# Three 2x2 block products with seven products each, in six of the eight ffn stages of a two-model transformer kernel

## The chip, the cores and the metric

The kernel runs on one core of a Trainium2 chip. The metric is the device time of one execution in microseconds (us); lower is better. A core has a matrix engine (PE, TensorE), two engines for elementwise work (DVE, VectorE, and ACT, ScalarE), GpSimd (POOL), a queue engine (SP, SyncE) that here only issues DMAs, and 16 DMA engines that all queues share.

## The reference, cut to what matters

The reference runs two small transformer models one after another on 256 tokens of width 1024, in float32: four blocks with eight feed-forward layers (ffn), and between these an HGRN2 mixer, forgetting attention (fox), a short convolution and sparse attention with compressed keys (kv, nsa). The change touches the ffn layers:

```python
def rmsnorm(x, g):
    y = x32 * lax.rsqrt(jnp.mean(x32 * x32, axis=-1, keepdims=True) + EPS)
    return (y * g.astype(jnp.float32)).astype(x.dtype)

def swiglu(h, w_in, w_out):
    gate, up = jnp.split(h @ w_in, 2, axis=-1)
    return (jax.nn.silu(gate) * up) @ w_out
...
x = x + 0.5 * swiglu(rmsnorm(x, norm_g[layer, 0]), ffn_w_in[layer, 0], ffn_w_out[layer, 0])
```

`w_in` is 1024 x 5632 (2816 gate columns, then 2816 up columns), `w_out` is 2816 x 1024.

## The kernel before, in words

The tokens are two tiles of 128 (t = 0, 1), the width is eight tiles of 128 (k). An ffn stage f (0 to 7) walks over 11 chunks c of 256 hidden columns. Each float32 factor is split in two parts, hi (rounded by ACT, `w_hi_`) and lo (the rest, subtracted by DVE, `w_lo_`), and a product is three matmuls: hi*hi, hi*lo, lo*hi.

One chunk is this:

- SP loads 2 MB of `w_in` (256 gate and 256 up columns) into `raw_in`, in halves of four k, as soon as the chunk in front has been split, and 1 MB of `w_out` into `raw_out`.
- ACT and DVE split each half (lines 435 and 445), 128x2048 elements at a time.
- PE does the first product for t = 0 and t = 1, 24 matmuls of 512 columns each, into `bank[t]` (lines 421 to 423).
- ACT takes silu of the gate half (line 792) and DVE multiplies it with the up half into `h_` (line 839; in the code `read(t)`). PE waits for the h of chunk c-1 before it writes the bank again.
- PE turns h by four transposes (`turn`, line 699), ACT and DVE split the turned h (lines 785 and 831), and `w_out` is split too (lines 798 and 844, `weights_out`).
- PE does the second product (`second`, 24 matmuls, lines 718 to 720), which adds into four accumulator banks. The second product of chunk c-1 comes behind the first product of chunk c.

Every engine runs its own list in the order in which the code is written, and waits on semaphores that others raise (`w_hi`, `w_lo`, `h`, `prod`, `ht_lo`, `wo_lo`). There is no scheduler. A load waits only for its buffer. At a stage's end the last chunk's `w_out` is split in halves (lines 814 and 859), and x is updated (line 868).

Of the kernel before, what the change touches and what calls it, by code (L numbers as in the profile page):

```python
# [8 lines left out]
ACT = mybir.ActivationFunctionType  # L9
# [5 lines left out]
P = 128  # L15
# [22 lines left out]
ARENA = 14336  # L38
# [34 lines left out]
M_FOX, M_NSA = 3 * NCH, 7 * NCH + 1  # L73

# [46 lines left out]
ns_csub ns_cexp ns_cp ns_cturned ns_cpt ns_cpv ns_co ns_turned13  # L121
own_act own_dve own_pool
# [21 lines left out]
class Memory:  # L144
    def __init__(self, nc, stack, t):
# [11 lines left out]
        self.wh = sb("w_hi_", [P, 2, KT, CW], F32R)  # L157
        self.wl = sb("w_lo_", [P, 2, KT, CW], F32R)
# [18 lines left out]
        self.lbs = sb("lower_bound_", [P, 2, KT])  # L177
        self.arena = sb("arena", [P, ARENA])
# [10 lines left out]
        for src, w in self.source:  # L189
            so_far = [so_far[p] + len(src(p)) for p in range(2)]  # L190
            self.land.append([16 * n for n in so_far])
# [16 lines left out]
    def piece(self, tile, n, half, k=None):  # L208

        w = self.source[n][1]  # L210
        if k is None:
            return tile[:, n % 2, 4 * half:4 * half + 4, 0:w]
        return tile[:, n % 2, 4 * half + k, 0:w]
# [131 lines left out]
def sp_program(g, sp):  # L345
    def chunk(n):
        if n == N_ALL:
            return
        src, w = g.source[n]
        for half in range(2):  # L350
            sp.wait_ge(g.w_lo, 8 * (n - 1) + 4 * half + 4)
# [6 lines left out]

    chunk(0)
    weights, f = ffn_weights(g.t), 0  # L360
    for s, kind in enumerate(STAGES):
        if kind == "ffn":
            w_out = weights[f][1].rearrange("(c k p) n -> c p k n", p=P, k=FC // P)
            for c in range(NCH):
                if f == 7 and c == 1:
                    sp.wait_ge(g.ns_turned, 2 * NSA_HEADS)
                if c:
                    out(m_of(f, c - 1), g.raw_out[:], w_out[c - 1])
                chunk(N0[s] + c + 1)
            out(m_of(f, NCH - 1), g.raw_out[:], w_out[NCH - 1])  # L370
# [6 lines left out]
        for c in range(CHUNKS[kind]):  # L377
            chunk(N0[s] + c + 1)
# [16 lines left out]
def pe_product(g, pe, n, t, out, u, w=CW, feature_major=False, slot=None, both=False):  # L395
# [3 lines left out]
    def operands(k):  # L399
        pe.wait_ge(g.w_lo, 8 * n + 4 * (k // 4) + 4)  # L400
        pe.wait_ge(g.xt_lo, 16 * u + pieces_for(u, t, k, feature_major, both))

    wh, wl, par = g.wh, g.wl, n % 2
    tok = slice(t * P, (t + 1) * P)
    mm = pe.e.matmul
    for f in range(2 if feature_major else 1):
        c = slice((2 * t + f) * P, (2 * t + f + 1) * P)
        for k in range(KT):
# [5 lines left out]
            if feature_major:  # L414
                o = out[:, f * T:(f + 1) * T]
                mm(o, wh[:, par, k, c], xt_hi[:, k, :], start=first, stop=False)  # L416
                mm(o, wh[:, par, k, c], xt_lo[:, k, :], start=False, stop=False)  # L417
                last = mm(o, wl[:, par, k, c], xt_hi[:, k, :], start=False, stop=end)  # L418
            else:
                o = out[:, 0:w]  # L420
                mm(o, xt_hi[:, k, tok], wh[:, par, k, 0:w], start=first, stop=False)  # L421
                mm(o, xt_hi[:, k, tok], wl[:, par, k, 0:w], start=False, stop=False)  # L422
                last = mm(o, xt_lo[:, k, tok], wh[:, par, k, 0:w], start=False, stop=end)  # L423
# [3 lines left out]
def act_split(g, act, n, half, k=None):  # L427
# [4 lines left out]
    act.wait_ge(g.prod, 2 * (n - 2) + 2)  # L432
# [5 lines left out]
def dve_split(g, dve, n, half, k=None):  # L438
# [3 lines left out]
    dve.wait_ge(g.w_hi, 8 * n + 4 * half + (4 if k is None else k + 1))  # L442
# [82 lines left out]
def act_high(g, act, s, t, half):  # L525
    act.wait_ge(g.scaled, 4 * S_FFN.index(s) + 2 * t + half + 1)
    act.wait_ge(g.prod, 2 * N0[s] - (1 if s == S_FFN[6] and t == 0 else 0))
    act.e.activation(g.xt_hi_[:, 4 * half:4 * half + 4, t * P:(t + 1) * P],
                     g.xg[:, half, :].rearrange("p (k n) -> p k n", k=4), ACT.Copy).then_inc(g.xt_hi, 4)


def dve_scaled(g, dve, s, t, half, gain):
    u = U[s]
    dve.wait_ge(g.turned, 4 * turned_before(u) + 2 * t + half + 1)
    dve.wait_ge(g.xt_lo, 4 * (4 * u + (half + 1 if t else 0)))
    by = g.gains[:, gain + 4 * half:gain + 4 * half + 4].unsqueeze(2).to_broadcast([P, 4, P])
    dve.e.tensor_tensor(g.xg[:, half, :].rearrange("p (k n) -> p k n", k=4),
# [3 lines left out]
def dve_low(g, dve, s, t, half):  # L541
# [3 lines left out]
    dve.e.tensor_tensor(g.xt_lo_[:, place[0], place[1]], g.xg[:, half, :].rearrange("p (k n) -> p k n", k=4),  # L545
# [18 lines left out]
def act_mixer_turn_x(g, act, s):  # L564
# [4 lines left out]
    act.wait_ge(g.prod, 2 * N0[s])  # L569
# [64 lines left out]
def act_turn_o(g, act, u, n, t, half):  # L634

    act.wait_ge(g.turned, 4 * turned_before(u) + 2 * t + half + 1)
    act.wait_ge(g.prod, 2 * n + t + 1)
# [34 lines left out]
def dve_out(g, dve, s, n):  # L672
    for c in range(2):
        def read(t):
            cols = slice(c * CW, (c + 1) * CW)
            dve.wait_ge(g.prod, 2 * (n + c) + t + 1)
# [3 lines left out]

def pe_ffn(g, pe, f, slot=None, chunks=1):
# [6 lines left out]
    def turn(c):  # L690
        if c == 0 and f == 0:
            pe.wait_ge(g.other_gains, 1)
        for t in range(NT):
# [1984 lines left out]
```

## Time and profile before

| | us |
|---|---|
| time, median of 3 executions (lowest, highest) | 2125.68 (2125.38, 2128.99) |
| span of the profiled execution, first to last instruction | 2123.9 |
| PE busy in the span | 2075.8 (98%) |
| DVE busy | 1196.0 (56%) |
| ACT busy | 1031.3 (49%) |
| POOL busy | 71.6 (3%) |

The profiled execution is known by its span alone; what lies around the span is the 1.8 us by which the median of the timed executions is above it. A share of 56% for DVE is a mean over stages. Matmuls overlap in the profile (each is shown with about 390 ns, while the next one starts about 227 ns later), so the pace of PE is read from starts and not from durations.

### The profile page before, as it was taken

What the parts mean: (1) busy time and instruction counts of PE and PEld (TensorE: products, weight loads), DVE (VectorE), ACT (ScalarE), POOL (GpSimd) and SP (SyncE); (2) the same over time, 40 slices, a digit from 0 to 9 for tenths busy, and PEclk for the clock granted to TensorE, in tenths of its full rate; (3) what the DMA queues carried; (4) which work ended last, traced back from release to release, by engine and by line L of the source; (5) the groups of instructions that cost most, each with busy time, mean ns of one, the idle gap of its engine ahead of it and who ended that gap; (6) DMA issues with size and microseconds to landing.
All of it is one profiled execution on the core that took longest, in us unless ns stands there. A gap on an engine that the chain in (4) does not pass through costs nothing.

```text
span 2123.9 us, 26075 instructions
## 1 busy us (share of the span) xinstructions
PE 2075.8 (98%) x10491; PEld 1744.1 (82%) x10491; DVE 1196.0 (56%) x1542; ACT 1031.3 (49%) x1359; POOL 71.6 (3%) x113
## 2 busy tenths in 40 slices
PE   8999999999999999999999999999999999989999
PEld 6887988888888878888888889888888787877887
DVE  5545687555645576654565446655555555765454
ACT  6435436444544468644454444544455444764443
POOL 2000000000000000000000000007001000000000
PEclk9999999999999999999999999999999999989999
DMA  8553425655555442565555544586647654114553
GB/s 260 191 195 120 159 91 173 212 179 191 175 196 193 140 159 80 178 218 179 178 178 180 197 158 159 188 244 195 179 138 173 204 191 168 62 57 162 178 180 117
DMA packets 259880, 359.98 MB, mean 169 GB/s; under 512 B 19582, under 2 KB 200234, under 8 KB 259760
## 3 DMA queue, kind: packets, MB, share of 16 engines
q1 hardware_dynamic: 256800, 351.57, 50.4%
q0 software_dynamic: 2016, 4.95, 1.5%
q10 hardware_dynamic: 944, 1.79, 0.3%
q8 instruction: 83, 1.36, 0.3%
q14 instruction: 37, 0.30, 0.0%
HBM read 356.70 MB, written 1.57 MB: 169 GB/s over the span
## 4 chain that ended last, share of the span: by engine, by line
PE 87%; DVE 6%; ACT 4%; issue 1%; DMA 1%; ACTq 0%; DVEq 0%; SPq 0%
PE bank L421 17%; PE bank L423 16%; PE bank L422 16%; PE acc L718 6%; PE acc L720 6%; PE acc L719 6%; PE bank L416 2%; PE bank L417 2%; PE bank L418 2%; PE tr L699 2%; DVE w_lo_ L445 2%; ACT w_hi_ L435 1%; PE acc L748 1%; PE acc L750 1%; PE acc L749 1%
## 5 line engine op out<-in xcount | busy, mean ns | idle before, releaser
L445 DVE TENSOR_TENSOR w_lo_<-raw_in,w_hi_ 128x2048 fp32r<-128x2048 f32 (+1 forms) x333 | 574.1, 1732 | 214.0 <-ACT w_hi_ L435 213.7
L421 PE MATMUL bank<-w_hi_,xt_hi_ 128*128 128x512 f32 x1648 | 658.4, 400 | 2.6 <-DVE xt_lo_ L545 2.4
L423 PE MATMUL bank<-w_hi_,xt_lo_ 128*128 128x512 f32 x1648 | 643.6, 391 | 0.0
L422 PE MATMUL bank<-w_lo_,xt_hi_ 128*128 128x512 f32 x1648 | 642.4, 390 | 0.0
L435 ACT ACTIVATE w_hi_<-raw_in 128x2048 fp32r<-128x2048 f32 (+1 forms) x333 | 481.7, 1461 | 64.7 <-DMA raw_in<-ffn_w_in 31.3
L844 DVE TENSOR_TENSOR wo_lo_<-raw_out,wo_hi_ 128x2048 fp32r<-128x2048 f32 x80 | 183.8, 2297 | 484.2 <-ACT wo_hi_ L798 484.2
L423 PEld LDWEIGHTS bank<-w_hi_,xt_lo_ 128*128 128x128 f32 x1648 | 309.4, 188 | 66.3
L421 PEld LDWEIGHTS bank<-w_hi_,xt_hi_ 128*128 128x128 f32 x1648 | 310.0, 188 | 64.9 <-issue 4.8
L422 PEld LDWEIGHTS bank<-w_lo_,xt_hi_ 128*128 128x128 f32 x1648 | 310.2, 188 | 59.0
L798 ACT ACTIVATE wo_hi_<-raw_out 128x2048 fp32r<-128x2048 f32 x80 | 153.3, 1916 | 369.7 <-PE acc L720 359.3
L718 PE MATMUL acc<-wo_hi_,ht_hi_ 128*128 128x512 f32 x576 | 224.3, 389 | 2.7 <-DVE ht_lo_ L831 2.7
L720 PE MATMUL acc<-wo_hi_,ht_lo_ 128*128 128x512 f32 x576 | 224.1, 389 | 0.0
L719 PE MATMUL acc<-wo_lo_,ht_hi_ 128*128 128x512 f32 x576 | 224.1, 389 | 0.0
L792 ACT ACTIVATE silu_<-bank,rstd_ 128x256 f32<-128x256 f32 x176 | 83.3, 473 | 221.0 <-PE bank L423 220.9
L718 PEld LDWEIGHTS acc<-wo_hi_,ht_hi_ 128*128 128x128 f32 x576 | 108.1, 188 | 25.9 <-DVE ht_lo_ L831 3.1
L720 PEld LDWEIGHTS acc<-wo_hi_,ht_lo_ 128*128 128x128 f32 x576 | 108.1, 188 | 22.5
L719 PEld LDWEIGHTS acc<-wo_lo_,ht_hi_ 128*128 128x128 f32 x576 | 108.1, 188 | 22.4
L839 DVE SCALAR_TENSOR_TENSOR h_tok<-bank,rstd_,silu_ 128x256 f32<-128x256 f32 x176 | 84.3, 479 | 72.5 <-ACT silu_ L792 72.4
L785 ACT ACTIVATE ht_hi_<-tr 128x512 fp32r<-128x512 f32 x80 | 47.9, 599 | 154.4 <-PE tr L699 154.4
L416 PE MATMUL bank<-xt_hi_,w_hi_ 128*128 128x256 f32 x352 | 101.9, 289 | 2.8 <-DVE xt_lo_ L604 2.8
L417 PE MATMUL bank<-xt_lo_,w_hi_ 128*128 128x256 f32 x352 | 99.6, 283 | 0.0
L418 PE MATMUL bank<-xt_hi_,w_lo_ 128*128 128x256 f32 x352 | 99.5, 283 | 0.0
(379 smaller groups left out, 2088.0 us busy)
## 6 DMA issues: line engine op xcount, KB each, us to landing
raw_in<-ffn_w_in SPq DMA_DIRECT2D x352, 512.0 KB, 4.9
raw_out<-ffn_w_out SPq DMA_DIRECT2D x88, 1024.0 KB, 5.0
raw_in<-hg_w_in SPq DMA_DIRECT2D x16, 1024.0 KB, 5.2
raw_in<-fox_w_in SPq DMA_DIRECT2D x16, 1024.0 KB, 5.4
raw_in<-conv_w_in SPq DMA_DIRECT2D x12, 1024.0 KB, 5.1
raw_in<-hg_w_out SPq DMA_DIRECT2D x4, 1024.0 KB, 5.0
raw_in<-fox_w_out SPq DMA_DIRECT2D x4, 1024.0 KB, 5.2
raw_in<-conv_w_out SPq DMA_DIRECT2D x4, 1024.0 KB, 5.0
```

Of the source, the lines that this page charges most:

```text
L416: mm(o, wh[:, par, k, c], xt_hi[:, k, :], start=first, stop=False)
L417: mm(o, wh[:, par, k, c], xt_lo[:, k, :], start=False, stop=False)
L421: mm(o, xt_hi[:, k, tok], wh[:, par, k, 0:w], start=first, stop=False)
L422: mm(o, xt_hi[:, k, tok], wl[:, par, k, 0:w], start=False, stop=False)
L423: last = mm(o, xt_lo[:, k, tok], wh[:, par, k, 0:w], start=False, stop=end)
L435: act.e.activation(g.piece(g.wh, n, half, k), raw, ACT.Copy).then_inc(g.w_hi, 4 if k is None else 1)
L445: dve.e.tensor_tensor(g.piece(g.wl, n, half, k), raw, g.piece(g.wh, n, half, k).bitcast(F32), ALU.subtract).then_inc(g.w_lo, 4 if k is Non ...
L718: mm(o, g.hth[:, at, :], g.oh[:, i, cols], start=(c == 0 and i == 0), stop=False)
L719: mm(o, g.hth[:, at, :], g.ol[:, i, cols], start=False, stop=False)
L720: ins = mm(o, g.htl[:, at, :], g.oh[:, i, cols], start=False, stop=False)
L798: act.e.activation(g.oh[:], g.raw_out[:], ACT.Copy).then_inc(g.wo_hi, 2)
L844: dve.e.tensor_tensor(g.ol[:], g.raw_out[:], g.oh[:].bitcast(F32), ALU.subtract).then_inc(g.wo_lo, 2)
```

## The change: what it does

In the stages f = 0, 1, 2, 3, 4 and 7 the chunks (2, 3), (5, 6) and (8, 9) are taken as pairs: 18 pairs. A pair's first product is a 2x2 block product: tokens t by k-halves on the side of x (A11, A12, A21, A22), and k-halves by gate/up, 512 columns each, on the side of the weights (B11, B12, B21, B22). It is computed with seven block products of 12 matmuls in place of eight (Strassen's form in Winograd's arrangement). This needs

- four sums of x blocks for each stage, 128x512 elements (`dve_x_add`), and their splits (`act_x_sum`, `dve_x_sum`), once in a stage, beside chunks 0 and 1;
- four sums of weight blocks for each pair, 128x2048 elements: T2, T4 and T1 by DVE in place (`dve_block_sum`), T3 = B12 + B22 by DVE in four pairs (the first ones of f = 0, 1, 3, 7) and by an accumulating DMA from GpSimd in the other fourteen (`pool_pairs`);
- seven splits of 128x2048 for each pair in place of four, on ACT (`act_block`) and on DVE (`dve_block`), of blocks or sums;
- sums of the product banks: one copy by ACT, seven adds of 128x512 by DVE, and two multiplications of 128x512 for h.

SP loads the four blocks (1 MB each) into an area that the mixers use too. The loads of a pair wait for splits of the pair before; in f = 0, 1, 3 and 7 the first pair's four loads stand ahead of chunk 1's. The two splits B11 and B21 and the sums T3, T2, T4 of a pair are done beside the single chunk in front of it. The second product of that chunk and of the one before are moved into the pair. A few constants (masks, the fox loads) are loaded later. The split buffers become a ring of four halves. All else of the computation is as before.

```diff
+PAIRED = {f: (2, 5, 8) for f in (0, 1, 2, 3, 4, 7)}
+PAIRS = [(f, c) for f in range(8) for c in PAIRED.get(f, ())]
+B11, B21, T2, T1, T3, B22, T4 = range(7)
+A_S1, A_S2, A_S3, A_S4 = range(4)
+T3_BY_POOL = [p for p, (f, c) in enumerate(PAIRS) if c != PAIRED[f][0] or f in (2, 4)]
...
+    def block(p, i):
+        f, c = PAIRS[p]
+        v = weights[f][0].rearrange("(k p) (g n) -> p k g n", p=P, g=2)
+        if p:
+            op = OPN[N0[S_FFN[PAIRS[p - 1][0]]] + PAIRS[p - 1][1]]
+            sp.wait_ge(g.w_lo, 4 * (op + (T1, T3, T4, B22)[i]) + 4)
+            sp.wait_ge(g.st_add, 3 * p)
+        sp.e.dma_start(g.blocks[i], v[:, i // 2 * 4:i // 2 * 4 + 4, i % 2, c * FC:(c + 2) * FC]).then_inc(
+            (g.b11_in, g.b12_in, g.b21_in, g.b22_in)[i], 16)
...
+def pe_pair(g, pe, f, p, turn, second, q, pending):
...
+    def product(bank, of_x, i):
+        op = OPN[n] + i
+        pe.wait_ge(g.w_lo, 4 * op + 4)
+        hi, lo = of_x
+        wh, wl, mm = g.wh[:, op % 4], g.wl[:, op % 4], pe.e.matmul
+        for k in range(KT // 2):
+            mm(bank[:], hi[:, k], wh[:, k], start=k == 0, stop=False)
+            mm(bank[:], hi[:, k], wl[:, k], start=False, stop=False)
+            last = mm(bank[:], lo[:, k], wh[:, k], start=False, stop=k == KT // 2 - 1)
+        last.then_inc(g.prod, 1)
...
+    product(z, x(0, 0), B11)
+    pe.wait_ge(g.h, 22 * f + 2 * q + 2)
+    product(y, x(1, 0), B21)
+    turn(q)
+    product(a, summed(A_S2), T2)
+    pe.wait_ge(g.st_cp, p + 1)
+    product(z, summed(A_S1), T1)
+    second(pending)
+    pe.wait_ge(g.st_c, 7 * p + 1)
+    product(y, summed(A_S3), T3)
+    pe.wait_ge(g.st_c, 7 * p + 2)
+    product(a, summed(A_S4), B22)
+    pe.wait_ge(g.st_c, 7 * p + 3)
+    product(z, x(1, 1), T4)
+    second(q)
...
+def dve_block(g, dve, p, i):
...
+    dve.e.tensor_tensor(g.wl[:, op % 4], g.block_of(i), g.wh[:, op % 4].bitcast(F32), ALU.subtract).then_inc(g.w_lo, 4)
...
+def dve_block_sum(g, dve, p, i):
...
+        dve.e.tensor_tensor(b12, b12, b22, ALU.add).then_inc(g.st_t3, 1)
...
+        dve.e.tensor_tensor(b11, b11, b12, ALU.add).then_inc(g.st_add, 1)
...
+        dve.e.tensor_tensor(b21, b21, b11, ALU.add).then_inc(g.st_add, 1)
...
+        dve.e.tensor_tensor(b11, b11, b22, ALU.subtract).then_inc(g.st_add, 1)
...
+def pool_pairs(g, pool, f):
...
+            pool.wait_ge(g.b12_in, 16 * (p + 1))
+            pool.e.dma_start(g.blocks[1], w[:, KT // 2:, 1, c * FC:(c + 2) * FC], accum_op=ALU.add).then_inc(g.t3_in, 16)
...
-        elementwise_chunk(g, dve, dve_split, n0 + c, read, slot_c, by_tile=bool(slot_c),
-                          between=(lambda: turn(c - 1)) if c else None)
+        if form == "S":
+            pair(PAIRS.index((f, c)), c - 1, pending)
+            pending = None
+        elif after == "S":
+            p = PAIRS.index((f, c + 1))
+            dve_block(g, dve, p, B11)
+            if pending is not None:
+                turn(pending)
+                weights_out(pending)
+            dve_block_sum(g, dve, p, T3)
+            dve_block_sum(g, dve, p, T2)
+            dve_block(g, dve, p, B21)
...
+                read(0)
+                dve_block_sum(g, dve, p, T4)
+            if c == PAIRED[f][0] - 1:
+                for i in range(4):
+                    dve_x_sum(g, dve, f, i)
+            read(1)
+            pending = c - 1
```

The list of DVE in stage f = 1, from the h of chunk 0, t = 0, before (L445 is a split of `w_in`, L839 is h, L844 the split of `w_out`, L831 that of the turned h):

```order
L839 SCALAR_TENSOR_TENSOR h_tok<-bank,rstd_,silu_ 128x256
L445 TENSOR_TENSOR w_lo_<-raw_in,w_hi_ 128x2048
L839 SCALAR_TENSOR_TENSOR h_tok<-bank,rstd_,silu_ 128x256
L844 TENSOR_TENSOR wo_lo_<-raw_out,wo_hi_ 128x2048
L445 TENSOR_TENSOR w_lo_<-raw_in,w_hi_ 128x2048
L831 TENSOR_TENSOR ht_lo_<-tr,ht_hi_ 128x512
L839 SCALAR_TENSOR_TENSOR h_tok<-bank,rstd_,silu_ 128x256
```

The same place now, from the h of chunk 0, t = 1 (L1273 is h; L1065 to L1074 are the x sums, L1003 a split of a weight block, L1016, L1020 and L1024 the sums T3, T2 and T4):

```order
L1273 SCALAR_TENSOR_TENSOR h_tok<-bank,rstd_,silu_ 128x256
L1065 TENSOR_TENSOR arena<-xt_full 128x512
L1068 SCALAR_TENSOR_TENSOR xt_full<-arena 128x512
L1071 TENSOR_TENSOR xt_full<-arena,xt_full 128x512
L1074 SCALAR_TENSOR_TENSOR arena<-arena,xt_full 128x512
L1003 TENSOR_TENSOR w_lo_<-arena,w_hi_ 128x2048
L1016 TENSOR_TENSOR arena<-arena 128x2048
L1020 TENSOR_TENSOR arena<-arena 128x2048
L1003 TENSOR_TENSOR w_lo_<-arena,w_hi_ 128x2048
L1273 SCALAR_TENSOR_TENSOR h_tok<-bank,rstd_,silu_ 128x256
L1024 TENSOR_TENSOR arena<-arena 128x2048
```

Between the h of chunk 0 (t = 1) and that of chunk 1 (t = 0) stood two 128x2048 operations and one of 128x512; now four of 128x2048 and four of 128x512 stand there. It goes on, on DVE, behind that T4 sum (L1053 are the splits of the x sums, L1029 is the sum T1, L1216 the split of the turned h, L1221 that of `w_out`, L1234 a sum of product banks):

```order
L1053 TENSOR_TENSOR sums_split<-arena,sums_split 128x512
L1053 TENSOR_TENSOR sums_split<-xt_full,sums_split 128x512 x2
L1053 TENSOR_TENSOR sums_split<-arena,sums_split 128x512
L1273 SCALAR_TENSOR_TENSOR h_tok<-bank,rstd_,silu_ 128x256
L1003 TENSOR_TENSOR w_lo_<-arena,w_hi_ 128x2048
L1029 TENSOR_TENSOR arena<-arena 128x2048
L1216 TENSOR_TENSOR ht_lo_<-tr,ht_hi_ 128x512
L1221 TENSOR_TENSOR wo_lo_<-raw_out,wo_hi_ 128x2048
L1003 TENSOR_TENSOR w_lo_<-arena,w_hi_ 128x2048
L1234 TENSOR_TENSOR silu_<-bank,arena 128x512
```

The L1273 row here is the h of chunk 1, t = 1, for which PE waits ahead of the product B21; the turned h of chunk 0, for which PE waits ahead of `turn(1)`, is split behind two more operations.

SP's list where the mixer in front of f = 1 ends, before (raw_in from hg_w_out is the mixer's last weight, then chunk 0 and chunk 1 of f = 1):

```order
L353 DMA raw_in<-hg_w_out 128x4x512 x4
L353 DMA raw_in<-ffn_w_in 128x4x256 x8
L357 DMA raw_out<-ffn_w_out 128x2x1024
L353 DMA raw_in<-ffn_w_in 128x4x256 x4
L357 DMA raw_out<-ffn_w_out 128x2x1024
```

and now:

```order
L431 DMA raw_in<-hg_w_out 128x4x512 x4
L431 DMA raw_in<-ffn_w_in 128x4x256 x4
L447 DMA arena<-ffn_w_in 128x4x512 x4
L431 DMA raw_in<-ffn_w_in 128x4x256 x4
L435 DMA raw_out<-ffn_w_out 128x2x1024
```

The four block loads of the first pair (L447) have moved in between chunk 0 and chunk 1.

## Rows read from the trace of the kernel before

**Rows 1.** The page: span, busy time, granted clock in 40 slices, chain by engine

```profile
span 2123.9 us, 26075 instructions
PE 2075.8 (98%) x10491; PEld 1744.1 (82%) x10491; DVE 1196.0 (56%) x1542; ACT 1031.3 (49%) x1359; POOL 71.6 (3%) x113
...
PEclk9999999999999999999999999999999999989999
...
PE 87%; DVE 6%; ACT 4%; issue 1%; DMA 1%; ACTq 0%; DVEq 0%; SPq 0%
```

**Rows 2.** Timeline of PE in stage f = 1: start us, duration us

```profile
371.78 0.39 PE L421 MATMUL bank<-w_hi_,xt_hi_ 128*128 128x512 f32 x1
...
377.22 0.60 PE L699 MATMUL tr<-ident,h_tok 128*128 128x128 f32 x4
377.57 0.48 PE L421 MATMUL bank<-w_hi_,xt_hi_ 128*128 128x512 f32 x1
...
383.15 0.39 PE L718 MATMUL acc<-wo_hi_,ht_hi_ 128*128 128x512 f32 x1
...
399.94 0.39 PE L718 MATMUL acc<-wo_hi_,ht_hi_ 128*128 128x512 f32 x1
```

**Rows 3.** Timeline of DVE, same stretch

```profile
370.44 2.29 DVE L445 TENSOR_TENSOR w_lo_<-raw_in,w_hi_ 128x2048 fp32r<-128x2048 f32 x1 [0.91 <-ACT w_hi_ L435]
372.65 0.48 DVE L839 SCALAR_TENSOR_TENSOR h_tok<-bank,rstd_,silu_ 128x256 f32<-128x256 f32 x1
...
376.69 2.29 DVE L445 TENSOR_TENSOR w_lo_<-raw_in,w_hi_ 128x2048 fp32r<-128x2048 f32 x1
378.90 0.68 DVE L831 TENSOR_TENSOR ht_lo_<-tr,ht_hi_ 128x512 fp32r<-128x512 f32 x1
379.50 0.47 DVE L839 SCALAR_TENSOR_TENSOR h_tok<-bank,rstd_,silu_ 128x256 f32<-128x256 f32 x1
```

**Rows 4.** Groups by line and shape: busy us, mean ns, idle before

```profile
L435 ACT ACTIVATE w_hi_<-raw_in 128x2048 fp32r<-128x2048 f32 x217 | 414.4, 1912 | 63.6 <-DMA raw_in<-ffn_w_in 31.3 <-PE bank L418 13.9 <-DMA raw_in<-conv_w_in 8.2
L868 DVE SCALAR_TENSOR_TENSOR x_tok<-acc,x_tok 128x512 f32<-128x512 f32 x32 | 22.0, 691 | 8.5 <-PE acc L750 8.4
L859 DVE TENSOR_TENSOR wo_lo_<-raw_out,wo_hi_ 128x1024 fp32r<-128x1024 f32 x16 | 19.6, 1226 | 33.9 <-ACT wo_hi_ L814 33.9
L814 ACT ACTIVATE wo_hi_<-raw_out 128x1024 fp32r<-128x1024 f32 x16 | 16.9, 1058 | 31.1 <-PE acc L750 31.1
```

**Rows 5.** Timeline of ACT: when chunk 1 is split, of f = 0, then of f = 1

```profile
19.75 2.18 ACT L435 ACTIVATE w_hi_<-raw_in 128x512 fp32r<-128x512 f32 x4
...
364.84 1.90 ACT L435 ACTIVATE w_hi_<-raw_in 128x2048 fp32r<-128x2048 f32 x1
...
368.43 1.91 ACT L435 ACTIVATE w_hi_<-raw_in 128x2048 fp32r<-128x2048 f32 x1
```

**Rows 6.** Windows: length, busy (x) PE, PEld, DVE, ACT, POOL, clock, DMA share, GB/s

```profile
0.00:10.00 10.00, 1.20 (x5) 1.04 (x6) 1.24 (x1) 4.74 (x5) 8.92 (x22) 1.00 0.82 268
...
15.00:20.00 5.00, 5.00 (x24) 4.12 (x23) 4.06 (x10) 3.38 (x10) 0.00 (x0) 1.00 0.91 283
20.00:25.00 5.00, 5.00 (x23) 3.94 (x22) 3.75 (x8) 4.97 (x9) 0.00 (x0) 1.00 0.87 321
```

**Rows 7.** The same view around the stretch where the clock falls

```profile
1860.00:1870.00 10.00, 6.44 (x37) 5.50 (x35) 6.71 (x24) 6.66 (x13) 0.91 (x2) 0.74 0.19 74
1870.00:1880.00 10.00, 9.00 (x41) 6.40 (x39) 4.41 (x21) 5.26 (x14) 0.45 (x1) 0.75 0.00 0
```

**Rows 8.** DMA issues: count, KB each, median us from issue to landing

```profile
raw_out<-ffn_w_out SPq DMA_DIRECT2D x88, 1024.0 KB, 5.0
...
arena<-cmp_w_k POOLq DMA_DIRECT2D x1, 1024.0 KB, 10.9
```

**Rows 9.** Timeline of SP and DVE at the end of the mixer in front of f = 1

```profile
343.67 14.61 SPq L353 DMA_DIRECT2D raw_in<-ffn_w_in  x8
...
343.56 0.68 DVE L677 TENSOR_TENSOR x_tok<-bank,x_tok 128x512 f32<-128x512 f32 x1
```

## What the change does to the time: the prediction

> **What bounds the kernel now.** The page comes first: PE is busy for 2075.8 of 2123.9 us, and the chain that ended last is 87% PE [rows 1]. So what counts is PE's own work, and every wait that is put into its list. Its timeline gives the pace: 24 matmuls of 512 columns stand between the starts 371.78 and 377.22, 0.2267 us each; the four transposes take 0.35; one whole chunk (48 first-product and 24 second-product matmuls, 4 transposes) lasts 399.94 - 383.15 = 16.79 us [rows 2]. The other engines are slack only as a mean: DVE 56%, ACT 49% [rows 1]. The pace of DVE is read from starts: 2.21 us for 128x2048 (376.69 to 378.90), 0.60 for 128x512 (378.90 to 379.50) [rows 3]; with a result of 128x512 out of a PSUM bank 0.69 from start to end [rows 4]. ACT takes 1.91 for 128x2048 [rows 4].
>
> **What is removed.** 12 matmuls for each of 18 pairs: 216 x 0.2267 = 49.0 us, 8.2 in each of the six stages, all on the path. That is the whole gain: no other engine loses work.
>
> **What is added on DVE.** For each pair three more splits (6.6 us), three sums of 128x2048 (6.6, and 2.2 more where T3 is DVE's), seven adds and two multiplications of 128x512 in place of four short ones (about 9 x 0.61 - 4 x 0.40 = 3.9): 17 us. In a stage 3 x 17 + 2.2 + eight operations for the x sums (5.4) = 59 us. The chunk had 3 x 2.21 + 0.60 + 2 x 0.40 = 8.0 us of DVE, 88 for 11 chunks. So DVE goes to about 147 us in a stage whose PE time falls from 11 x 16.8 = 185 to 177: 83%, and among the pairs 3 x 8.0 + 17 = 41 of 3 x 16.8 - 2.7 = 47.7, 86% without a single wait. With an in-order list that is close enough to full for the order to count. I walk through it place by place, the clock at zero where chunk 0's first product ends on PE (371.78 in stage 1, [rows 2]).
>
> *Place 1, the h of chunk 1.* PE: chunk 1's product with a turn lasts 383.15 - 371.78 = 11.4 us [rows 2], then B11 12 x 0.2267 = 2.7, and at 14.1 PE waits for the h of chunk 1 (t = 1), ahead of B21. DVE comes free at 372.65 + 0.40, that is 1.3 [rows 3]. Then it does four x sums, each waiting for the one in front (0.69 + 0.1 for the semaphore, rows 3 and 4 for the duration: 3.1), the split B11 (2.2), T3 (2.3), T2 (2.2), B21 (2.2), one h (0.4), T4 (2.2), four splits of x sums (2.4), the last h (0.5) = 17.5. It ends at 18.8: PE waits 4.7 us. Where T3 is the DMA's (f = 2, 4) 2.3 less: 2.4. The second product of chunk 0, which covered this place before (5.4 us), now comes behind it.
>
> *Place 2, the turned h.* PE does B21 (2.7) and waits for the turned h of chunk 0; DVE does the split T2, the sum T1 and that split: 2.2 + 2.3 + 0.7 = 5.2. Wait 2.5. *Place 3, T1.* PE turns and does T2 (3.2); DVE splits `w_out` and T1 (4.5). Wait 1.3. From there second(0) covers 5.4 us. *Later pairs:* no x sums; DVE is just behind, about 1.1 us for the two.
>
> *Place 4, the stage's end.* `w_out` of chunk 9 is split later than before (behind the first product's half of chunk 10), so SP asks for chunk 10's `w_out` only then. Counted from the end of second(8): transposes and ACT's turned h 1.1, ACT 1.9, DVE 2.3, landing 5.0 [rows 8], ACT half 1.06, DVE half 1.23 [rows 4], the last split and semaphores 1.0 = 13.6; PE has 5.9 + 2.7 + 0.2 + 2.7 + 0.2 = 11.7. Wait 1.9.
>
> So a stage waits 4.7 + 2.5 + 1.3 + 1.1 + 1.9 = 11.5 us where 8.2 are gained, and 9.2 in f = 2 and 4.
>
> **What is moved: chunk 1 behind four block loads.** In f = 0, 1, 3, 7 they are 4.2 MB in SP's queue ahead of chunk 1. The rate when the queue is full is 283 to 321 GB/s [rows 6]. *f = 0:* up to chunk 1's first half there are chunk 0 (2.1), the blocks (4.2), the half (1.05), x (1.05) and constants (0.6), 9.0 MB. 2.7 are there after 10 us [rows 6], the rest takes 21 at 0.30, and the landing 1.5: 32.5, against a split that begins at 19.75 [rows 5] and a product that begins at about 24.7 (chunk 0's end). With the first pieces of the split 33.9: wait 9, and 1 more for the second half: 10. *f = 1 (and 3):* from 343.67 [rows 9] chunk 0, the blocks and half a chunk are 7.35 MB, 23.0 us at 0.32, and 1.7 to land: 368.4 instead of 364.84, the second half at 371.7 instead of 368.43 [rows 5]. The splits stand ahead of h on ACT and DVE, so place 1 begins 3.3 us later; all of it counts: 3.3. *f = 7:* the blocks wait for the x of the nsa stage, which comes at its very end and not 12 us earlier (343.56, [rows 9]): 5.1.
>
> Sum over the stages: f = 0: 11.5 + 10 - 8.2 = +13.3; f = 1, 3: 11.5 + 3.3 - 8.2 = +6.6 each; f = 2, 4: +1.0 each; f = 7: +8.4. Together +36.9.
>
> **The clock.** The granted clock is the full 2.4 GHz nearly all the time [rows 1]. Once it fell to half, in the stretch 1860 to 1880, where PE was busy 6.44 of 10 us [rows 7]: at half speed a product of 12 costs 2.7 more. Here PE stands for 5 to 10 us in four stages. From nothing (no fall) to 10 us (some 5 us at half speed, six or more products, twice hidden); I take 5. The Trainium skill, "TensorE: Matmul & The Clock Gate", section "Part 1: The HAM clock gate", says that being idle throttles the clock and activity frees it: by it nearly each of these waits costs something, which is the upper end. The row above agrees.
>
> **The accumulating DMA.** Nothing of the kind is in the trace. It is issued when B12 has landed, about 14 us before DVE needs T3 (between: the rest of a pair and its last products). Nearest rows: a plain load of 1 MB from SP's queue 5.0, one from POOL's 10.9 us, in 512-byte pieces [rows 8]. It reads what it adds to and shares the engines with 4 MB of other loads, so twice the lower is likely: 10, hidden. Were it 5 or 11 the sum is the same. Beyond 14, each us costs up to one for each of the 12 pairs that have no other stage between. The Trainium skill, "DMA: Bandwidth & Descriptors", section "Anatomy of one DMA — SWDGE (gpsimd) path", has 2.0 us plus the bytes by 436 GB/s for a DMA from GpSimd: 4.4 us, an estimate by that page, which leaves the sum as it is.
>
> Masks and the fox loads move to where nothing waits for them: 0; if that cover is gone, at most the 5.0 us of a plain landing each [rows 8].
>
> **Sum.** 2123.9 + 36.9 + 5 = 2166, and 1.8 around the span, as in the median before: **2168 us**, 2% slower.
>
> **Rivals.**
> - *DVE keeps up (faster).* If the x sums and block sums run in DVE's idle time, places 1 to 3 vanish: -49 + 1.9 x 6 + 11 (the late loads, of which half stay) = about -27: 2099. It decides at place 1: the wait must be under 1 us, so DVE's chain under 14 us in place of 17.5. For it: 56% mean load, and some 100 us of idle DVE in each stage. Against it: the list above fixes these operations between two h, and their starts are measured. 9%.
> - *No change:* waits and gains meet at 49, if the loads of the blocks come with no delay (-22) and the clock does not fall (-5), and later places are half as long (-14): 2126. 4%.
> - *The accumulating DMA is late (slower still).* Its descriptors are made by GpSimd, and it reads and writes. At 17 us DVE waits 2.7 us in 12 pairs, and PE with it: +32, 2200; at 20 us 2235. For it: POOL's plain load took 10.9 with less beside it. The Trainium skill, "SBUF — State Buffer", section "Who interferes with whom", says that DVE operations with two SBUF inputs hold up GpSimd's reads; no row here shows it. 17%.
> - *Forecast:* 70%, between 2140 and 2195.
>
> **Numbers.** Low end 2138: without the clock and with the late loads at a third. High end 2212: the late DMA at 18 us. Outside lie 10% below and about 10% above. What a measurement of this kernel can tell from no change is about 0.2% (4 us). Faster by more 9%, within 4%, slower 87%.
>
> **What would show it.** The chain of waits with PE waiting for h before B21, 5 to 8 us in f = 0, 1, 3, 7 and 2 to 3 in f = 2, 4; for the turned h 2.5 and for the split T1 1.3 in all six; 1.9 at the end of a stage; in f = 0 a gap of some 9 us before chunk 1. DVE without a gap from chunk 0's h to the end of the first pair. T3's DMA landing in 8 to 13 us with nobody waiting. I am wrong if DVE idles at place 1, if T2's sum waits for the DMA, or if the clock falls for longer than the waits.

## The result and the profile after

The changed kernel takes 2159.95 us (median, 2158.78 to 2160.44) against 2127.34 (2125.38 to 2130.02) for the kernel before in the same runs: ratio 1.0154, 95% interval 1.014 to 1.0168, so 1.5% slower. The profiled execution has a span of 2157.5 us. The page, the lines that answer to the first two of [rows 1]:

```profile
span 2157.5 us, 26237 instructions
PE 2058.4 (95%) x10275; PEld 1713.5 (79%) x10275; DVE 1544.1 (72%) x1792; ACT 1145.0 (53%) x1419; POOL 89.5 (4%) x127
```

The 216 matmuls are gone (10491 to 10275). Two differences carry the result, both read from the two profiled executions. PE's time without work is 2157.5 - 2058.4 = 99.1 us, before 2123.9 - 2075.8 = 48.1: **51.0 us of new waits**. And its busy time fell by only 17.4 where 49.0 us of products left it: **31.6 us in which the same work took longer**. -49.0 + 51.0 + 31.6 = +33.6, the change of the span.

The view of PE's waits (engine, line waited for, releaser: us in total, times, longest). L838 is the first matmul of a pair's product, L560 of a chunk's, L884 the turning of h, L961 the last chunk's second product. The rows left out between them (`tr<-DVE diag_` 8.9, `tr<-DMA arena<-norm_g` 5.8) are in the kernel before too, with 8.9 and 6.1:

```profile
PE bank L838 <- DVE h_tok L1273: 27.0, 6, 5.8
...
PE acc L961 <- DVE ht_lo_ L1342: 7.4, 6, 1.5
PE bank L560 <- DVE h_tok L1273: 7.3, 2, 6.3
...
PE tr L884 <- DVE ht_lo_ L1216: 4.5, 3, 2.2
PE tr L838 <- DVE w_lo_ L1003: 3.9, 4, 1.0
```

More than half of the new waits is the first place: PE stands for the h of chunk 1 ahead of B21. DVE's timeline in f = 1 from chunk 0's two h to that h (start us, us; the answer to [rows 3]):

```profile
384.10 0.48 DVE L1273 SCALAR_TENSOR_TENSOR h_tok<-bank,rstd_,silu_ 128x256 f32<-128x256 f32 x1
385.49 2.29 DVE L585 TENSOR_TENSOR w_lo_<-raw_in,w_hi_ 128x2048 fp32r<-128x2048 f32 x1 [0.91 <-ACT w_hi_ L575]
387.70 0.48 DVE L1273 SCALAR_TENSOR_TENSOR h_tok<-bank,rstd_,silu_ 128x256 f32<-128x256 f32 x1
388.09 0.68 DVE L1065 TENSOR_TENSOR arena<-xt_full 128x512 f32<-128x512 f32 x1
...
390.87 2.28 DVE L1003 TENSOR_TENSOR w_lo_<-arena,w_hi_ 128x2048 fp32r<-128x2048 f32 x1
393.08 2.28 DVE L1016 TENSOR_TENSOR arena<-arena 128x2048 f32<-128x2048 f32 x1
395.39 2.29 DVE L1020 TENSOR_TENSOR arena<-arena 128x2048 f32<-128x2048 f32 x1
397.60 2.28 DVE L1003 TENSOR_TENSOR w_lo_<-arena,w_hi_ 128x2048 fp32r<-128x2048 f32 x1
399.81 0.47 DVE L1273 SCALAR_TENSOR_TENSOR h_tok<-bank,rstd_,silu_ 128x256 f32<-128x256 f32 x1
400.20 2.28 DVE L1024 TENSOR_TENSOR arena<-arena 128x2048 f32<-128x2048 f32 x1
402.40 0.68 DVE L1053 TENSOR_TENSOR sums_split<-arena,sums_split 128x512 fp32r<-128x512 f32 x1
...
404.81 0.47 DVE L1273 SCALAR_TENSOR_TENSOR h_tok<-bank,rstd_,silu_ 128x256 f32<-128x256 f32 x1
```

There is no gap: the four sums over x, B11, T3, T2, B21, one h, T4, four splits, the last h, 17.2 us from 388.09 on. PE's timeline where it gets that h, then goes on:

```profile
405.33 0.80 PE L838 MATMUL bank<-w_hi_,xt_hi_ 128*128 128x512 f32 x1 [5.81 <-DVE h_tok L1273]
405.93 0.63 PE L839 MATMUL bank<-w_lo_,xt_hi_ 128*128 128x512 f32 x1
406.35 0.63 PE L840 MATMUL bank<-w_hi_,xt_lo_ 128*128 128x512 f32 x1
406.78 0.63 PE L838 MATMUL bank<-w_hi_,xt_hi_ 128*128 128x512 f32 x1
...
410.46 0.66 PE L884 MATMUL tr<-ident,h_tok 128*128 128x128 f32 x4
...
414.95 0.47 PE L838 MATMUL tr<-w_hi_,sums_split 128*128 128x512 f32 x1 [1.03 <-DVE w_lo_ L1003]
...
424.71 0.39 PE L838 MATMUL bank<-w_hi_,sums_split 128*128 128x512 f32 x1
...
426.81 0.39 PE L838 MATMUL bank<-w_hi_,sums_split 128*128 128x512 f32 x1
...
437.10 0.39 PE L560 MATMUL bank<-w_hi_,xt_hi_ 128*128 128x512 f32 x1
...
439.14 0.39 PE L560 MATMUL bank<-w_hi_,xt_hi_ 128*128 128x512 f32 x1
```

Two parts of the 31.6 us can be read here. *The clock:* B21's twelve matmuls last from 405.33 to 410.46, 5.1 us in place of 2.7; after the wait they start 0.43 us apart, which is 512 columns at 1.2 GHz. The windows (length, busy of PE, PEld, DVE, ACT, POOL, clock, DMA share, GB/s) say the same, for the stretch with the wait and the one behind it (from 403.00 to 405.30 alone, with PE still standing, the granted clock is 0.51):

```profile
400.00:410.00 10.00, 4.67 (x11) 3.74 (x12) 9.97 (x10) 2.07 (x3) 0.00 (x0) 0.66 0.00 0
410.00:420.00 10.00, 8.95 (x40) 6.74 (x40) 10.00 (x7) 8.60 (x7) 0.00 (x0) 1.00 0.62 228
```

Counted over the timeline of the whole run, 65 of 7018 distances between the starts of neighbouring matmuls of 512 columns lie between 0.38 and 0.52 us, before 3 of 7234: 62 x 0.20 = 12 us. The first steps of six such stretches (0.58 to 0.60 where a step behind a wait is 0.34 at full speed) bring the clock's part to an estimated 14 us. Seven of the stretches belong to the pairs' stages: behind the wait for chunk 1 in f = 0, in B21 in f = 0, 1, 3 and 7, and in T2 in f = 2 and 4.

*The pair products' pace:* nine matmuls from 424.71 to 426.81 start 0.2333 us apart, nine of a chunk from 437.10 to 439.14 start 0.2267 apart. Over the whole run the distances under 0.30 us are 6 us longer in sum, most of it in the products that read `sums_split` (0.2333 on average). Some 11 us, steps at bank changes and behind waits among them, are not assigned.

The DMA issues (count, KB, median us to landing):

```profile
arena<-ffn_w_in SPq DMA_DIRECT2D x72, 1024.0 KB, 6.0
...
arena<-ffn_w_in POOLq DMA_DIRECT2D x14, 1024.0 KB, 12.7
```

The accumulating DMA takes 11.1 to 13.7 us and nobody waits for it. By stage, from the start of the first of its last four `x_tok` operations (before 198.1, 544.0, 732.2, 1078.5, 1266.7, 1798.8, 2119.1 in f = 0, 1, 2, 3, 4, 6, 7; after 210.8, 562.7, 752.0, 1105.0, 1294.6, 1825.4, 2152.6), the loss is 12.7 us in f = 0, then +6.0, +1.1, +6.7, +1.4, over the two stages without pairs -1.3, and +6.9 in f = 7.

### The profile page after: what moved, and what is told of

Its sections match the earlier page's. It is cut to its first block and busy times, and to the rows that moved or that the text cites. A ratio compares the mean times of both kernels' runs of the same rounds, so it can differ in the third digit from the quotient of the medians.

```text
span 2157.5 us, 26237 instructions
## 1 busy us (share of the span) xinstructions
PE 2058.4 (95%) x10275; PEld 1713.5 (79%) x10275; DVE 1544.1 (72%) x1792; ACT 1145.0 (53%) x1419; POOL 89.5 (4%) x127
## 5 line engine op out<-in xcount | busy, mean ns | idle before, releaser
L585 DVE TENSOR_TENSOR w_lo_<-raw_in,w_hi_ 128x2048 fp32r<-128x2048 f32 (+1 forms) x261 | 409.5, 1579 | 158.5 <-ACT w_hi_ L575 158.3
L560 PE MATMUL bank<-w_hi_,xt_hi_ 128*128 128x512 f32 x1072 | 433.1, 404 | 10.5 <-DVE h_tok L1273 7.3
L562 PE MATMUL bank<-w_hi_,xt_lo_ 128*128 128x512 f32 x1072 | 419.9, 392 | 0.0
L561 PE MATMUL bank<-w_lo_,xt_hi_ 128*128 128x512 f32 x1072 | 418.9, 391 | 0.0
L575 ACT ACTIVATE w_hi_<-raw_in 128x2048 fp32r<-128x2048 f32 (+1 forms) x261 | 344.1, 1337 | 79.8 <-DMA raw_in<-ffn_w_in 32.7
L1003 DVE TENSOR_TENSOR w_lo_<-arena,w_hi_ 128x2048 fp32r<-128x2048 f32 x126 | 288.1, 2286 | 30.1 <-ACT w_hi_ L995 30.1
L1221 DVE TENSOR_TENSOR wo_lo_<-raw_out,wo_hi_ 128x2048 fp32r<-128x2048 f32 x80 | 183.4, 2293 | 165.6 <-ACT wo_hi_ L1104 165.4
L995 ACT ACTIVATE w_hi_<-arena 128x2048 fp32r<-128x2048 f32 x126 | 237.9, 1906 | 42.8 <-DVE arena L1029 41.4
L560 PEld LDWEIGHTS bank<-w_hi_,xt_hi_ 128*128 128x128 f32 x1072 | 202.4, 189 | 52.9 <-DVE h_tok L1273 8.7
L562 PEld LDWEIGHTS bank<-w_hi_,xt_lo_ 128*128 128x128 f32 x1072 | 201.9, 188 | 43.8
L561 PEld LDWEIGHTS bank<-w_lo_,xt_hi_ 128*128 128x128 f32 x1072 | 202.7, 189 | 37.3
## 6 DMA issues: line engine op xcount, KB each, us to landing
arena<-ffn_w_in POOLq DMA_DIRECT2D x14, 1024.0 KB, 12.7
```

What stands on the lines that cost most here:

```text
L560: mm(o, xt_hi[:, k, tok], wh(k)[:, 0:w], start=first, stop=False)
L561: mm(o, xt_hi[:, k, tok], wl(k)[:, 0:w], start=False, stop=False)
L562: last = mm(o, xt_lo[:, k, tok], wh(k)[:, 0:w], start=False, stop=end)
L575: act.e.activation(g.piece(g.wh, n, half, k), raw, ACT.Copy).then_inc(g.w_hi, 4 if k is None else 1)
L585: dve.e.tensor_tensor(g.piece(g.wl, n, half, k), raw, g.piece(g.wh, n, half, k).bitcast(F32), ALU.subtract).then_inc(g.w_lo, 4 if k is Non ...
L995: act.e.activation(g.wh[:, op % 4], g.block_of(i), ACT.Copy).then_inc(g.w_hi, 4)
```

## The experiments

Each is one edit of the changed kernel (2159.95), except where it says more; the kernel before measured 2126.1 to 2127.2 beside each.

**Without pairs.** `PAIRED = {}`, all else stays, but for one wait of GpSimd's that took its count from the table of pairs.

> All code of the change stays in the program (the moved constants, the buffers of the pairs, the split helper), but the table of pairs is empty, so every chunk is computed as before. My theory is that all of the loss is in the pairs' own waits at their edges: this must be the kernel before, 2126 within 3 us. Rival: the new layout of the buffers or the moved constants costs something by itself: 2130 or more. From the difference to the changed kernel (2160) the pairs' sum is read: about 49 us of products saved and about 82 us given back.

2125.29 (ratio to the kernel before 0.9996, 0.9987 to 1.0005). Layout, constants and the moved loads cost nothing.

**The block loads behind chunk 1's.**

```diff
-                block(p, 0)
-                block(p, 1)
...
-                    if c == 0 and here:
-                        block(p, 3)
-                        block(p, 2)
                     i += 1
                     chunk(i)
+                    if c == 0 and here:
+                        for which in (0, 1, 3, 2):
+                            block(p, which)
```

> The first pair's four block loads of f = 0, 1, 3, 7 are issued behind chunk 1's instead of ahead of it; nothing else changes. Theory (DVE's chain starts late because chunk 1 lands late): the whole 18 to 22 us of the term come back, so about 2140 (ratio to before 1.006); in f = 0 the wait of 6.3 before chunk 1 goes, and the stage ends some 10 us earlier; in f = 1 and 3 DVE is free 1.3 us after chunk 0's end instead of 3.4, so 2 us each; f = 7 some 4. Rival (the blocks are then late themselves, and DVE idles at the sum T3): under 8 us come back, 2152 or more, and the wait before B21 grows. Rival (the loads don't count, only the order on DVE): no change, 2160.

2145.62 (1.0095, 1.008 to 1.011): 14.3 less, where 18 to 22 were expected. In f = 0 PE's wait of 6.28 us ahead of chunk 1 is gone; the first place keeps most of its waits (25.4 us in all, 27.0 in the changed kernel), and its longest, in f = 0, grew from 5.3 to 6.8:

```profile
PE bank L837 <- DVE h_tok L1272: 25.4, 6, 6.8
```

So the late loads are a cost of their own, and DVE's list at the first place is another.

**The four sums over x by GpSimd** (`dve_x_add` as `pool.e.tensor_tensor` on GpSimd's queue, one of them with its sign turned, which the later add takes up).

> The four sums of x blocks of a stage (3.1 us of DVE, between the two h) are done by GpSimd, with one sign turned so that plain adds and subtractions do; DVE keeps all else. Theory (what stands on DVE between the h of chunk 0 and that of chunk 1 sets PE's wait): the wait before B21 falls by 3 us, from 5.8 to 2.8 in f = 1, 3, 7, 5.3 to 2.3 in f = 0, 2.1 to 0 in f = 2, 4 (where the rest shows at the turned h): 14 to 18 us less, 2142 to 2146. Rival (DVE is not what holds PE there, it is the landing of the blocks): no change. Rival (GpSimd and DVE stand in each other's way in SBUF): DVE's operations beside the four get longer, and little or nothing is gained.

2148.67 (1.0106, 1.0091 to 1.0121): 11.3 less, under the 14 to 18 expected. The first place falls from 27.0 to 15.2 us, but the wait for the turned h grows from 4.5 to 7.4. In f = 1 the four adds fall into a gap of DVE's, and no operation of DVE's is longer there. The two waits:

```profile
PE bank L838 <- DVE h_tok L1280: 15.2, 6, 4.7
...
PE tr L884 <- DVE ht_lo_ L1223: 7.4, 5, 2.2
```

**T3 never by DMA, T3 always by DMA.**

The first run and the second each change one line:

```diff
-T3_BY_POOL = [p for p, (f, c) in enumerate(PAIRS) if c != PAIRED[f][0] or f in (2, 4)]
+T3_BY_POOL = []
```

```diff
-T3_BY_POOL = [p for p, (f, c) in enumerate(PAIRS) if c != PAIRED[f][0] or f in (2, 4)]
+T3_BY_POOL = [p for p, (f, c) in enumerate(PAIRS)]
```

> All 18 sums T3 are done by DVE, no accumulating DMA. Theory (DVE is full all through the pairs): 14 more operations of 2.2 us on DVE, 2.2 x 2 in the first pairs of f = 2, 4 and most of 2.2 in the twelve later pairs, 25 to 31 us more: 2185 to 2191. Rival (the later pairs have slack, PE sets the pace there): only f = 2, 4 lose, +5: 2165. Rival (the accumulating DMA, 12.7 us from issue to landing, costs others more than it saves): faster than 2160.

> All 18 sums T3 come from the accumulating DMA, also in the first pairs of f = 0, 1, 3, 7. Theory: DVE's chain between the two h gets 2.3 us shorter in four stages and the DMA, issued when B12 lands, 12.7 us to landing, is in time in f = 1 and 3 but just late in f = 0 and 7: -5 to -9 us, 2151 to 2155. Rival (the DMA is late in all four, since it can't start before B12 has landed and DVE wants T3 some 9 us after): slower, 2165 or more, with DVE idle before T2's sum.

Never: 2200.58 (1.0353, 1.0335 to 1.037), 40.6 more for 14 sums of 2.3 us = 32. The theory named the right mechanism, but its 2185 to 2191 was some 10 us too low. In the profiled execution, 35.3 us longer than the changed kernel's, PE stands 25.8 us more and is 9.5 us longer at its work, at a mean clock of 0.982 in place of 0.986. The waits it makes are in the second and third pairs, where there were nearly none:

```profile
PE bank L838 <- DVE h_tok L1273: 32.0, 6, 6.0
PE acc L903 <- DVE ht_lo_ L1216: 26.0, 13, 2.0
```

Always: 2172.72 (1.0218, 1.0203 to 1.0233), 12.8 more. The time is that of the rival, the mechanism isn't: DVE stands nowhere ahead of T2's sum, so the DMA was in time. The first place does fall, to 15.1 us, yet nothing is won. ACT's timeline in f = 1 shows why, the first half of chunk 1's weights, in the changed kernel and then here, with PE's wait below it:

```profile
379.88 1.92 ACT L575 ACTIVATE w_hi_<-raw_in 128x2048 fp32r<-128x2048 f32 x1 [2.24 <-DMA raw_in<-ffn_w_in]
```

```profile
389.08 1.91 ACT L575 ACTIVATE w_hi_<-raw_in 128x2048 fp32r<-128x2048 f32 x1 [8.18 <-DMA raw_in<-ffn_w_in]
...
PE bank L560 <- DVE h_tok L1273: 27.7, 4, 10.0
```

The program is 3.3 us later by then (the last operations of f = 0 start at 214.0 against 210.8), the weights 9.2. The DMA is in time for T3 but shares the DMA engines with the loads of chunk 1. They are full here (share 1.05 and more) from 370 to 390, in the changed kernel only until 380. PE's wait ahead of chunk 1 rises from 7.3 to 27.7 us, four waits of 4.8 to 10.0.

**Both edits that helped.**

> Both of the earlier edits at once: the first pair's block loads behind chunk 1's, and the four sums over x by GpSimd. Apart they gave 14.3 and 11.3 us. Theory: chunk 1 is late for two reasons that follow each other (its weights come late, then VectorE reaches its h late), so once the weights are in time the rest of the wait is VectorE's, and the two gains add up nearly: 2134 to 2138. Rival: the two cover each other (both only move chunk 1's end): no better than the better one alone, 2145.

2140.64 (1.0062, 1.0049 to 1.0075): 19.3 less than the changed kernel, of the 25.6 that the two gave apart. The time lies between the two theories, nearer to the sum.

**The blocks behind, and the sums over x left out.** In the five stages behind the first, the four sums work on one column, on DVE (their result is left out).

> As x_blocks_behind, and in the five stages behind the first the four sums over x work on one column only (their result is left out of the computation), on VectorE as in the changed kernel: the sums cost nearly nothing and no GpSimd work stands beside VectorE. Beside x_behind_and_gpsimd (2140.6) this tells what GpSimd's adds cost VectorE. In that run's trace VectorE's low part beside GpSimd's adds takes 3.37 us against 2.29 alone, 1.1 us in each stage. Theory, contention: 4 to 8 us under it, 2133 to 2137. Rival, the adds on GpSimd cost nothing and the first pair's own chain sets the wait: within 2 us of 2140.6.

2139.57 (1.0061, 1.0048 to 1.0073), 1.1 from the run with GpSimd's adds: the rival was right. DVE's timeline in f = 1:

```profile
380.48 0.16 DVE L1074 SCALAR_TENSOR_TENSOR arena<-arena,xt_full 128x1 f32<-128x1 f32 x1
381.24 2.29 DVE L1002 TENSOR_TENSOR w_lo_<-arena,w_hi_ 128x2048 fp32r<-128x2048 f32 x1 [0.60 <-ACT w_hi_ L994]
```

With the sums gone DVE waits for ACT's B11, which stands behind chunk 0's silu; that split begins at 381.24 here and at 381.39 in the run above. Once DVE is free of them, the sums cost nothing more that these times show.

**The splits of the sums by GpSimd too**, on top of x_behind_and_gpsimd.

```diff
-    dve.e.tensor_tensor(g.sal[i], g.sa_raw_of(i)...
+    pool.e.tensor_tensor(g.sal[i], g.sa_raw_of(i)...
```

> As x_behind_and_gpsimd, and the four low parts of the sums over x, which VectorE computes right ahead of chunk 1's h, also by GpSimd. In the trace of the changed kernel they hold VectorE 2.4 us ahead of that h in each stage. If VectorE's queue at the first place is what TensorE waits for, 2.4 us less in four stages and about 2 in the two others: 12 to 14 us under x_behind_and_gpsimd, about 2122 to 2126, level with the kernel before. Rival: TensorE then waits for the turned h behind it (the second place), and only half comes back: 2129 or more.

2145.21 (1.0091, 1.0076 to 1.0107): 4.6 *more*. The theory was wrong, and of the rival only the wait for the turned h came, not the half that was to be won. 2.4 us left DVE's list ahead of h, and the list got no shorter (DVE, and one of the four rows of GpSimd beside it):

```profile
384.05 2.28 DVE L1015 TENSOR_TENSOR arena<-arena 128x2048 f32<-128x2048 f32 x1
386.36 3.28 DVE L1019 TENSOR_TENSOR arena<-arena 128x2048 f32<-128x2048 f32 x1
389.56 3.38 DVE L1002 TENSOR_TENSOR w_lo_<-arena,w_hi_ 128x2048 fp32r<-128x2048 f32 x1
392.86 0.47 DVE L1283 SCALAR_TENSOR_TENSOR h_tok<-bank,rstd_,silu_ 128x256 f32<-128x256 f32 x1
393.26 2.98 DVE L1023 TENSOR_TENSOR arena<-arena 128x2048 f32<-128x2048 f32 x1
396.16 0.47 DVE L1283 SCALAR_TENSOR_TENSOR h_tok<-bank,rstd_,silu_ 128x256 f32<-128x256 f32 x1
...
387.46 3.33 POOL L1063 TENSOR_TENSOR sums_split<-xt_full,sums_split 128x512 fp32r<-128x512 f32 x1
```

GpSimd runs its four splits from 385.88 to 397.35. Beside them DVE's operations with two SBUF inputs take 3.28, 3.38 and 2.98 us in place of 2.28, while those that read a PSUM bank stay at 0.47: 2.8 us lost for 2.4 saved. GpSimd pays too: such an operation takes 3.33 us here and 1.29 where DVE has no such operation beside it. Behind this place DVE's next split still takes 2.96, and the wait for the turned h rises from 6.3 to 13.2 us in all, while the first place falls only from 15.9 to 13.1. The Trainium skill, "SBUF — State Buffer", section "Who interferes with whom", says that a DVE instruction with two SBUF inputs contends with a GpSimd one that reads SBUF, and one with a single SBUF input does not; this trace agrees.

**More of that kind**, on top of x_gpsimd_splits_too: T4's sum in later pairs by GpSimd, and in first pairs the second product ahead of T1 on PE (and the turned h ahead of T1's sum on DVE).

> As x_gpsimd_splits_too, with two more edits: in the second and third pair the fourth weight sum (the one over B22 and B11's neighbour, a 128x2048 add of 2.2 us) by GpSimd, and in the first pair of a stage the turned h of the chunk ahead stands before the product T1 on TensorE and its turning before T1's sum on VectorE. Theory: the wait at the first place is then covered by the turned h's product, another 6 to 12 us: 2110 to 2118, under both kernels. Rival: GpSimd's adds of 128x2048 take longer than TensorE's product that covers them, or slow VectorE at their shared port, and the time stays at 2124 or above.

2136.1 (1.0043, 1.0031 to 1.0056): better than all runs with pairs above, but still behind the kernel before. The 2110 to 2118 expected did not come, the rival's 2124 or more did. Of its two grounds GpSimd's row shows the first, what the sum costs it (2.28 us on DVE); which of the edits gave what was not tried apart:

```profile
L1057 POOL TENSOR_TENSOR arena<-arena 128x2048 f32<-128x2048 f32 x12 | 79.1, 6590 | 238.7 <-DVE w_lo_ L1006 238.7
```

**Two pairs a stage, at chunks 5 and 8**, the block loads behind chunk 3's.

> Two pairs in each of the six stages, at chunks 5 and 8, none at chunk 2; the first pair's block loads stand behind chunk 3's. Twelve pairs save 12 x 2.72 = 33 us of products. Theory: the waits at the start of a stage (chunk 1's late weights, the h of the chunk ahead of the first product, VectorE behind by chunk 0's and the sums' work) belong to a pair that comes right behind the stage's start, so the trace shows no wait of over 1 us of TensorE on h ahead of the first pair; what is left is one place at each pair of about 2 to 3 us and 1.2 us at the stage's end, 5 to 6 us a stage, and the time is level with the kernel before: 2123 to 2130. Rival: VectorE is full wherever a pair stands, so the wait on h moves with the first pair to chunk 4's end and stays at 4 to 6 us: 2138 or more.

2135.72 (1.0037, 1.0023 to 1.005), between the two theories. The wait on h ahead of the pairs is gone in all stages, and so is the late chunk 1; left are the turned h and the stage's end:

```profile
PE tr L883 <- DVE ht_lo_ L1215: 13.7, 6, 2.3
...
PE acc L960 <- DVE ht_lo_ L1341: 8.8, 6, 2.8
```

By the page PE is busy 2061.0 of 2134.1 us, 25.0 us more without work than before. 144 matmuls (32.7 us) are gone, so it is 2061.0 - (2075.8 - 32.7) = 17.9 us longer at its work. -32.7 + 25.0 + 17.9 = +10.2. The expectation counted the waits and left out the second part. The wait of 2.3 us has another cause than a full DVE: ACT splits T2 only when chunk 4's silu is done, and DVE stands 0.82 and 1.39 us here.

```profile
436.15 0.47 ACT L1139 ACTIVATE silu_<-bank,rstd_ 128x256 f32<-128x256 f32 x1 [3.36 <-PE bank L561]
436.52 1.91 ACT L994 ACTIVATE w_hi_<-arena 128x2048 fp32r<-128x2048 f32 x1
```

**The clock kept up.** In the changed kernel, PE passes the wait at the first place with products nobody reads.

```diff
     product(z, x(0, 0), B11)
+    if c == PAIRED[f][0]:
+        pe.wait_ge(g.h, 22 * f + 2 * q + 1)
+        pe.wait_ge(g.w_lo, 4 * (OPN[n] + B21) + 4)
+        beside, wh = x(0, 0)[0], g.wh[:, (OPN[n] + B21) % 4]
+        for k in range(8 if f in (2, 4) else 20):
+            pe.e.matmul(a[:], beside[:, k % 4], wh[:, k % 4], start=True, stop=True)
```

> The changed kernel, and in each stage's first pair TensorE passes the wait for h at the first place with 20 products more (8 in f = 2 and 4) into a bank that the next product overwrites; nothing else is moved, the output is the same. In the changed kernel's trace the four long waits (5.3 to 5.8 us) are each followed by about 12 products at 0.43 us in place of 0.227, 2.4 us more. Theory: VectorE's list sets the end of this stretch, so the slow product only covers the wait for the turned h, which is there in f = 2 and 4 (2.17 and 2.13 us) and missing in the four others; with the clock kept up that wait comes back and the time stays: 2156 to 2161. Rival: what the clock takes adds to the waits: 4 x 2.4 us and what is behind it less, 2146 to 2150.

2161.53 (1.0167, 1.0152 to 1.0182): the theory was right, half a us above its range. PE in f = 1:

```profile
400.95 4.87 PE L855 MATMUL bank<-w_hi_,xt_hi_ 128*128 128x512 f32 x20 [0.82 <-DVE h_tok L1279]
405.95 0.50 PE L838 MATMUL bank<-w_hi_,xt_hi_ 128*128 128x512 f32 x1
...
408.59 0.39 PE L840 MATMUL bank<-w_hi_,xt_lo_ 128*128 128x512 f32 x1
411.08 0.66 PE L890 MATMUL tr<-ident,h_tok 128*128 128x128 f32 x4 [2.10 <-DVE ht_lo_ L1222]
411.49 0.62 PE L838 MATMUL bank<-w_hi_,sums_split 128*128 128x512 f32 x1
```

B21 now takes 2.9 us at full speed, and the wait for the turned h is there, 2.10 us (12.7 in the six stages, 4.5 in the changed kernel). After that wait the clock falls for T2 instead, in all stages but f = 2. At this place the clock's loss and the wait are the same time, spent either way.

**A plain operand.** The four products that read sums over x read a tile of plain x instead (result left out).

> The changed kernel with the four products of a pair that read the sums over x reading a tile of the plain turned x instead (the sums are still made and waited for, the result is not the reference's). In the changed kernel's trace these products start 0.2333 us apart, the chunks' own 0.2267. Theory: the distance comes with the operand's place in memory (the sums lie in a buffer of their own): with plain x it is 0.227 and the 864 products give 5 to 6 us back, about 2154. Rival: it comes from what the other engines do beside the pair, or from the alternation of the banks: the distance stays 0.233 and the time 2160.

2157.1 (1.0145, 1.0128 to 1.0162): 2.9 less, where 5 to 6 were expected; the lowest and highest times of the two kernels nearly touch (2158.48, 2158.78), so the trace must decide. In it the distance belongs to the operand: the same products average 0.2268 to 0.2286 by line, and the distances under 0.30 us are 5.8 us shorter in sum. Most of that is not won: 80 distances are at half speed in place of 65 (3 us), and PE stands 1.2 us more (the first place 28.4, T1 6.2 us).

## Why the prediction was right, and where only its sum was

The direction and the mechanism came as forecast: DVE's list makes PE wait at the named places, and that costs more than the products save. The sizes of the terms are another matter.

**Removed work.** 216 x 0.2267 = 49.0 us, as counted.

**Place 1.** DVE's chain was put at 17.5 us and is 17.2. With the late loads PE's wait was 4.7 + 3.3 = 8.0 in f = 1 and is 5.81. PE itself was later too: its list from the end of chunk 0 (384.63) to the wait (399.52) is 14.9 us, not 14.1, and DVE began its chain 3.5 us behind that end, where 1.3 + 3.3 had been counted. f = 2 and 4: 2.4 predicted, 2.13. f = 7: with its 5.1 us of late loads, for which the prediction shows no working, 9.8 were due and 1.05 + 5.83 came.

**Place 2** is mis-sized: 2.5 us in six stages was predicted; it stands in f = 2 and 4 (2.17, 2.13) and is missing in the four others (0.2 us in one), because B21 ran at half speed there and took the same 2.4 us. **Place 3:** 1.3 in all six was predicted; it is 0.86 to 1.03 in those four and missing in f = 2 and 4, where T2 ran at half speed. So two of the signs said to stand in all six stages do not. **Later pairs:** 1.1 predicted; in f = 1 0.65. **Place 4:** 1.9 predicted, 1.03 to 1.46.

**Late chunk 1.** f = 0: 10 predicted, 6.28 measured in one wait, with some 3 us of slow matmuls behind it (the stage lost 12.7 where 13.3 was said). x_blocks_behind gave 14.3 of the 21.7 us counted for all four stages.

**The clock** was taken as 5 us with 10 as the upper end; it is about 14. The five waits of 5.3 to 6.3 us are each followed by matmuls at 1.2 GHz, and so are the two waits of 2.17 and 2.13 for the turned h (f = 2, 4), each with only B21 between it and a wait of 2.13; the waits of 0.9 to 1.5 us at places 3 and 4 are not. Against it stand 51.0 us of waits where the places and loads added up to 49.0 + 36.9 = 85.9. That is the larger error, 35 us, and it is nearly made good by the 31.6 us of slower work, of which 5 were in the sum. At place 2 the two errors belong together, as x_kept_warm shows: the slow product fills the stretch in which PE would have waited. For the rest this was not tried, and that the sum comes out so near is in part luck. By stage the sum without the clock was +13.3, +6.6, +1.0, +6.6, +1.0, +8.4, and came out +12.7, +6.0, +1.1, +6.7, +1.4, +6.9. The forecast of the span was 8.3 us too high: 5 are the clock's, counted on top of waits that it fills; 2.1 lie in the six stages, most of them in f = 7; 1.3 come from the two stages without pairs.

**Not foreseen:** the pair products' pace, about 6 us.

**The range.** The low end of 2138 doesn't follow from its two grounds: 2168 - 5 - 14.5 = 2148.5. And the two rivals below it, with 9% and 4%, are more than the 10% that it leaves. Neither touches the forecast.

**The accumulating DMA:** 10 us estimated, 12.7 measured (longest 13.7) within a cover put at 14; nobody waits for it. The trace does not agree with the 4.4 us that went by the Trainium skill, "DMA: Bandwidth & Descriptors", "Anatomy of one DMA — SWDGE (gpsimd) path". The rival of the late DMA was wrong for this kernel. In x_t3_all_dma, too, it is in time, and what it costs there are the loads beside it.

**The rival "DVE keeps up"** decided at the wait of place 1 being under 1 us. x_two_later_pairs has no such wait at all, and is still slower than before: the turned h, the stage's end and the slower work are left.

No version with pairs beats the kernel before. The best two stay 0.4% behind.

## What to carry to other kernels

A form with fewer products moves work to the elementwise engines. Count that work in the order of their lists, from one operand that PE waits for to the next, and not as a share of the span: DVE was busy 56% of the time before and 72% after, and was still what PE waited for. A wait on PE and the slow matmuls behind it can be one account, as at place 2 here: predict when the chain of the other engine ends, not the wait plus a clock term. Before an add is moved to GpSimd, look what DVE does at that moment: between operations with two SBUF inputs the exchange may lose, as it did with the splits.

## What the hardware showed that I had not expected

- An accumulating DMA of 1 MB issued by GpSimd lands after 11.1 to 13.7 us, a plain one of the same size from SP's queue in the same stages after 6.0 (median); its issue holds GpSimd 1.3 us. With four more of them, chunk 1's weights in f = 1 came 9.2 us later, in a program that was 3.3 us later by then.
- GpSimd's tensor_tensor of 128x2048 takes 6.59 us (mean), DVE's 2.28; beside GpSimd's 128x512 splits DVE's takes 2.98 to 3.38, and the splits themselves up to 3.33 (1.29 for the same shape with no such operation of DVE's beside it).
- The same matmul starts 0.2333 us apart with one stationary operand and 0.2267 with another, and with the second in the first one's place the difference is gone (x_plain_operand). Why the buffer matters stays open: place, layout and order of reading were not tried apart.
